# Start of the expert stage of a hybrid attention and mixture-of-experts block: when the eighth place's weights are asked for, how the first place is refilled, and one dummy run on TensorE

## The reference, cut to what matters

```python
def hier_moe(x2, w_group, b_group, w_router, b_router, w1, w3, w2):
    # per token: the best of 4 groups, then the best 2 of its 8 experts
    gate = p_g[:, None] * top_p / jnp.sum(top_p, axis=-1, keepdims=True)
    expert = g_idx[:, None] * EXP_PER_GROUP + top_i
    ...
    # per expert, for the tokens that chose it
    hb = jax.nn.silu(xb @ w1[e]) * (xb @ w3[e])
    return (hb @ w2[e]) * gte[:, None]
```

## Time and profile before

| what | value |
|---|---|
| median of three executions | 1028.24 us (1027.07 to 1031.07) |
| the profiled execution's own time | 1029.96 us |
| its span, first to last instruction | 1028.2 us |
| mean granted clock of TensorE | 0.989 |
| PE busy | 982.1 us, 96% |
| DVE, ACT, POOL busy | 517.1, 342.7, 39.8 us |
| read from HBM | 259.60 MB |
| chain that ended last | PE 74%, DMA 14%, DVE 5%, ACT 4% |

### The profile page before, as it was taken

One profiled execution on the slowest core, in us unless ns is written; L12 is line 12 of the kernel. 1 busy time (PEld: TensorE's weight loads), 2 busy tenths in 40 slices (PEclk: granted clock), 3 DMA queues, 4 the chain that ended last, 5 costly groups with the idle time before them and its releaser, 6 DMA issues.

```text
span 1028.2 us, 12797 instructions
## 1 busy us (share of the span) xinstructions
PE 982.1 (96%) x4953; PEld 624.7 (61%) x4953; DVE 517.1 (50%) x949; ACT 342.7 (33%) x691; POOL 39.8 (4%) x61
## 2 busy tenths in 40 slices
PE   8999999999999999999996999999999889898995
PEld 6778877867788898888884344444443333333342
DVE  5369799777466356545347133333332223333326
ACT  6332356767862354444243111111111110111113
POOL 1000000000000000000001000000000000000000
PEclk9999999999999999999998999999999999999998
DMA  8422322121123535323399999999999999999993
GB/s 242 133 83 82 90 75 83 41 83 42 42 82 117 210 103 185 123 83 123 111 357 350 397 396 426 428 428 425 426 426 426 426 428 427 426 427 421 422 416 131
DMA packets 67744, 260.73 MB, mean 254 GB/s; under 512 B 11697, under 2 KB 39394, under 8 KB 52194
## 3 DMA queue, kind: packets, MB, share of 16 engines
q1 hardware_dynamic: 63266, 248.08, 61.1%
q0 software_dynamic: 3248, 7.87, 2.1%
q10 hardware_dynamic: 1168, 3.93, 1.0%
HBM read 259.60 MB, written 4.19 MB: 257 GB/s over the span
## 4 chain that ended last, share of the span: by engine, by line
PE 74%; DMA 14%; DVE 5%; ACT 4%; issue 3%; ACTq 0%; DVEq 0%; POOLq 0%
PE ps L2144 16%; PE ps L1808 13%; PE ps L1810 13%; PE ps L1809 13%; DMA eraw<-in_w 12%; PE ps L2197 8%; PE ps L2207 2%; PE ps L2208 2%; PE ps L2122 1%; DVE s L1364 1%; DMA xrows<-xf 1%; PE ps L1983 1%; DVE nmax L1366 1%; PE ps L2184 1%; ACT whi L981 1%
## 5 line engine op out<-in xcount | busy, mean ns | idle before, releaser
L2144 PE MATMUL ps<-eraw,XT 128*64 128x512 f32 x984 | 228.0, 603 | 10.5 <-DMA eraw<-in_w 10.5
L2144 PEld LDWEIGHTS ps<-eraw,XT 128*64 128x64 f32 x984 | 67.6, 138 | 131.9 <-issue 128.3
L1315 DVE TENSOR_TENSOR wlo<-raw,whi 128x2048 fp32r<-128x2048 f32 (+2 forms) x43 | 95.9, 2230 | 80.7 <-ACT whi L981 80.6
L1655 DVE TENSOR_TENSOR h<-ps,h 128x512 f32<-128x512 f32 x128 | 79.5, 683 | 84.6 <-PE ps L2208 84.6
L2197 PE MATMUL ps<-eraw,HT 128*64 128x512 f32 x512 | 113.1, 593 | 5.4 <-issue 5.4
L1808 PE MATMUL ps<-xT_hi,whi 128*128 128x512 f32 (+1 forms) x256 | 103.7, 405 | 1.4 <-DVE xT_lo L1322 1.4
L1810 PE MATMUL ps<-xT_hi,wlo 128*128 128x512 f32 (+1 forms) x256 | 100.1, 391 | 0.0
L1809 PE MATMUL ps<-xT_lo,whi 128*128 128x512 f32 (+1 forms) x256 | 100.0, 390 | 0.0
L981 ACT ACTIVATE whi<-raw 128x2048 fp32r<-128x2048 f32 (+2 forms) x43 | 80.2, 1865 | 45.3 <-PE ps L1810 45.3
L2197 PEld LDWEIGHTS ps<-eraw,HT 128*64 128x64 f32 x512 | 38.5, 137 | 77.5 <-issue 77.5
L1155 ACT ACTIVATE HT<-ps 128x512 f32<-128x512 f32 x15 | 9.0, 597 | 191.7 <-PE ps L2184 191.7
(11 more groups left out here) (346 smaller groups left out, 1602.9 us busy)
## 6 DMA issues: line engine op xcount, KB each, us to landing
eraw<-in_w SPq DMA_DIRECT2D x64, 2048.0 KB, 28.6
eraw<-in_w SPq DMA_DIRECT2D x61, 1024.0 KB, 13.4
raw<-in_w_in SPq DMA_DIRECT2D x9, 1024.0 KB, 5.0
raw<-in_w_gate SPq DMA_DIRECT2D x8, 1024.0 KB, 5.4
raw<-in_w_ckv SPq DMA_DIRECT2D x8, 1024.0 KB, 5.2
raw<-in_w_out SPq DMA_DIRECT2D x4, 1024.0 KB, 5.1
raw<-in_w_cq SPq DMA_DIRECT2D x4, 1024.0 KB, 5.0
raw<-in_w_co SPq DMA_DIRECT2D x4, 1024.0 KB, 5.0
```

Source lines behind the costliest of these rows:

```text
L1315: dve.tensor_tensor(wlo[n % 2][:, 0:w], raw[n % RING][:, 0:w], whi[n % 2][:, 0:w].bitcast(f32), ALU.subtract).then_inc(w_lo, 1)
L1655: dve.tensor_tensor(v, ps[bank][:, :], v, ALU.add).then_inc(comb_added, 1)
L2144: ins = pe.matmul(ps[1 + c // 2][rows, :], XT[p % 2][:, kk, rows], unit_rows(2 * p + m, c, k), start=(kk == 0), stop=(kk == KT - 1))
```

## The change

Place 7 waits for the first exponential of the gates in place of the last tile of xf. The first place is refilled in three DMAs per unit, rows 0:1, 1:2 and 2:4, where it was two; the first two of them wait for k = 0 and k = 1 of the first part, and both units' pieces alternate. The dummy runs behind the table of token numbers are four, where they were three.

```diff
     SPARED = SEQ_W[8]
+    REFILL_ROWS = [slice(0, 1), slice(1, 2), slice(2, 4)]
...
-                    take([unit], [slice(0, 2), slice(2, 4)] if took[0] in (2 * NS, 2 * NS + 1) else [None])
+                    take([unit], REFILL_ROWS if took[0] in (2 * NS, 2 * NS + 1) else [None])
...
-    LOADS[REFILL:REFILL + 4] = [LOADS[REFILL + i] for i in (0, 2, 1, 3)]
+    LOADS[REFILL:REFILL + 6] = [LOADS[REFILL + i] for i in (0, 3, 1, 4, 2, 5)]
...
-            sp.wait_ge(n_out, OUT_UPTO["h1"] + TT)
+            sp.wait_ge(route_exp, 1)
             load_place(7)
...
             for n in range(REFILL, len(LOADS)):
-                if n < REFILL + 2:
-                    sp.wait_ge(rows_used, 2)
+                if n < REFILL + 4:
+                    sp.wait_ge(rows_used, 2 * LOADS[n][-2].stop)
                 else:
                     sp.wait_ge(e_wused, LOADS[n][-1])
...
                     ins.then_inc(full(*s), 1)
-                    stay_awake(3)
+                    stay_awake(4)
...
                         if k == 3:
                             ins.then_inc(e_wused, 1)
-                        elif (p, c, k) == (0, 0, 1):
+                        elif (p, c) == (0, 0) and k < 2:
                             ins.then_inc(rows_used, 1)
```

## The result

The changed kernel's median is 1031.95 us (1028.02 to 1033.72, 18 executions), that of before, measured beside it, 1028.16 us (1026.84 to 1031.33, 18). The ratio is 1.0025, with a 95% interval from 1.0015 to 1.0035: **slower by about 2.6 us**. The ratio is not the quotient of the two medians, which lie 3.8 us apart. The loss is within the half per cent that the prediction called "same", but it has the other sign than its 1025.7 us, and it lies outside its range of 1023.4 to 1029.4. The profiled execution took 1030.74 us, with a span of 1029.0 us.

The account below looks back on a forecast made before the run. The weight stream, dry near 610 us and anchored to TensorE's start, bounds the end; 1.0 us (gather) plus 1.57 (clock), 2.55 rounded, gives 1027.4 for the profiled execution, 1025.7 on the median; range 1023.4 to 1029.4.

Parts of the forecast that it names:

- same: Outcome class for the whole kernel: within about 0.5%, 5.1 us, of no change; chance 0.92.
- The anchor: Weight stream dry near 610 us, its next load waiting on TensorE, so the end hangs on TensorE's start.
- 1.6 us of missing stream: Between 608 and 616 us the weight stream was said to lack 664 KB against 424 GB/s.
- Place 7 behind the exponential: Before the gather: later loads let the last store land about 549 to 550, ending the gather's wait 1.24 us earlier.
- The gather itself: Ahead of the transposes: issued at 553.74, taking 4.35 us for 4.11, so TensorE starts 1.0 us earlier.
- far bound: Longest duration considered for the gather: 8.0 us, that of a gather amid a full stream.
- The slower rival: Place 7's load and the spare unit reach into the gather, 8.0 us: 1030.9, deciding from 5.35 us; chance 0.10.
- the bound drawn from it: At the gather: engines taking turns among queues limit its delay to the spare unit's remainder, far from 8.0 us.
- The clock: At transposes and first experts: idle time shrinks to about 1.1 us, full clock saves 1.57 us, bounds 0 and 1.57.
- The fourth dummy: Ahead of the table of gates: the added dummy run is covered by TensorE's 1.17 us wait for DVE, cost 0.
- the six pieces: First place's refill starts 0.86 us sooner, taken up by the dry stream at 612: gain 0, bounds +0.86 and -0.3.
- The 0.5% band: For the whole kernel's time: about 0.5%, 5.1 us, is what a measurement can tell from no change.

Follow-up runs that it names:

- fifth kernel: The changed kernel with the ninth place's load waiting until the gather has landed; median 1029.72 us, ratio 1.0003 against the kernel before.
- first kernel: The kernel before with only place 7's new wait, for the first exponential; median 1031.58 us, ratio 1.0021.
- seventh kernel: The kernel before with five dummy runs in place of two behind the table of gates, ahead of the transposes; median 1028.39 us, ratio 0.9987.
- second kernel: The kernel before with only the first place's refill in three row pieces per unit; 1029.19 us, ratio 1.0009.
- third: The kernel before with only the added dummy run, four in place of three; 1027.82 us, ratio 0.9991.
- twelfth kernel: The kernel before with place 7's new wait, half the spare unit's loads behind the gather's begin and four dummies, not two, ahead of the transposes; 1027.75 us, ratio 0.9990.
- eleventh: The changed kernel with half the spare unit's loads behind the gather's begin and four dummies, not two, ahead of the transposes; 1027.85 us, ratio 0.9997 against before.
- fourth: The changed kernel with all four spare unit loads behind the gather's begin, ahead of the ninth place; 1027.81 us, ratio 0.9995 against before.

## Why the prediction was wrong

**The anchor** was right. The stream is dry near 610 us, and TensorE's start passes through it to the last parts one for one, to some tenths (fourth column). Its 1.6 us of missing stream are too many, though: in rows 3 the engines are full from 608 to 612 (share 1.08) in spite of 334 GB/s. The idle engine time of rows 5, at a share of 0.39 over 1.2 us, is 0.7 us.

**Place 7 behind the exponential** was right in every step but its worth. The issue went out at 546.19 (546.1 forecast), the store landed at 550.1 (549 to 550), x_at took over the gather's wait, and the gather was issued at 553.89 (553.74).

**The gather itself is the step that failed.** The prediction took 4.35 us, with 8.0 us as the far bound for a gather amid a full stream. Measured are 6.22, 8.02, 6.11 and 6.85 us in four kernels, and 5.65 with nothing behind it. Two prices in the step were wrong.

The first is that of the queue ahead. The queue itself was nearly as supposed. At the gather's issue 1.18 MB stood ahead of it (fifth kernel), where it was 0.41 MB before; at 424 GB/s that is 2.8 against 1.0 us of stream, of which 1.25 us is the earlier issue (553.73 against 554.98) and the rest the load that was put off. But in these traces the gather's first packets move only 1.6 to 2 us behind its issue, and from then on 0.43 MB of the queue were left, 1.0 us of stream (fifth kernel, from 555.7), against 0.04 MB before (from 556.6): 0.9 us more of shared engines, where the step said 0.7. It charged 0.25 us for them, and they cost 1.5.

The second price was left out: that of the ninth place's load, asked for 1.3 us behind the gather's issue. The prediction named this load only to set it aside, since it comes behind. It reaches the engines while the gather's last packets are still under way; in the first kernel 1.08 MB of weights moved while ten packets were outstanding (from 559 us), in the changed one 0.49 MB beside the last eleven. Before, nearly all of the gather had moved when that load's packets came: only 13 of its packets were left at 558 us, where the changed kernel had 32.

The slower rival named the place and the point of decision, 5.35 us, and priced it at 1030.9; it was given 0.10, and the range left it out. The row of 8.0 us should have been taken as the near one: the two gathers between 575 and 600 us, amid a full stream, take 7.7 to 8.7 us in every one of these traces, while the 4.11 us were measured on one that the late store had kept waiting until the queue was nearly empty. The rule of the Trainium skill (DMA: Bandwidth & Descriptors, queues, rings and completion order) that engines take turns among queues with work is not contradicted. But rows 8 don't test it, since 153 packets of the store beside 405 of loads are not even turns, unless the store's queue was often empty. And the bound drawn from it, a delay of no more than the remainder of the spare unit, left out what is asked for later and gives no price for the tail: in the fifth kernel the gather is still moving after 558 us, at a DMA share of 0.12.

**The clock** was right in size and wrong in direction. The 1.57 us were predicted for a start at full against one at half clock; the seventh kernel, whose edit does nothing but keep TensorE busy, gains 1.3 us by its ratio, 0.9987 (0.2 to 2.5 us by its interval), and its 64 records take 13.95 us (13.90 forecast, 14.59 before). But the idle stretch was to shrink to 1.1 us and grew to 2.94. The second kernel, whose edit comes into play only later, stood idle 2.19 us at the same place and was granted full clock at 559.0 to 562.4, where before it was half after 2.06 us. In the fourteen traces the idle stretch ahead of the transposes was at most 1.38 us in six, and none of them shows half clock there; it was 1.76 to 4.74 us in eight, and seven do. The Trainium skill (TensorE: Matmul & The Clock Gate, Part 1) says that the monitor behind the clock runs freely; the prediction concluded that the fall need not come in every execution, and the trace of the second kernel, with full clock, agrees. That the same kernel has executions with and without the price, and that a later gather makes more of them pay, fits these traces, but was not shown on several of one kernel.

**The fourth dummy and the six pieces** at nothing were right, by the traces of the third, second and twelfth kernels. The 0.5% band was right too.

What stays open: why the last few packets take so much longer in one execution than in another (6.11 to 8.02 us with the ninth place's load behind them), and how the loss splits between the loads ahead and behind in a typical execution; one profile per kernel can't tell.

## What to carry to other kernels

A transfer that is put off to clear the way for one thing is still to be made: ask what it then meets, and price the next small transfer on the critical path at its duration in a full queue, not at the one it had while something else kept it waiting. Loads asked for behind it count too, since its last packets can be overtaken. Where a stream of loads has a dry stretch, everything ahead of it that only fills the queue earlier is worth nothing, and what holds back the compute engine counts in full; moving loads to protect a gather helps only until the dry stretch is used up.

If this start is to be improved, the cheap part is the clock: three dummy runs while TensorE waits, a ratio of 0.9987 (0.9976 to 0.9998), the only one whose interval lies below 1, and by little: it is one of twelve, and was measured beside the highest median of the kernel before, 1029.40. The eleventh and twelfth kernels have medians of 1027.85 and 1027.75, as low as any (1027.81 and 1027.82 in the fourth and third), and no execution above 1029.8 in 24, but their intervals include 1, and that they beat the seventh was not shown.

## What the runs showed of the hardware that was not expected

A gather of 0.23 MB that finds a busy queue when it starts is not made good when the queue drains: in the fifth kernel all engines together were busy 0.47 of the time from 557 to 558 us and 0.12 from 558 to 559.3, and it landed only at 559.37. With a load coming behind it, ten packets of 0.01 MB took the last 2.6 us (first kernel). A store of 512 KB issued in the same instant as 1 MB of loads took 10.2 us, and with 2 MB 9.9; put off those loads by 1.9 us, and it took 5.8.
